# Second half of the output projection and second norm by token tile, two U blocks ahead of query 0, norm weights and keys loaded at the end of the heads

## What is computed

```
x = x + mix @ w_out[l]
x = x + peer_ffn(rms_norm(x, norm2_g[l]), peer_wq[l], peer_keys[l], peer_u[l], peer_v[l])
```

## Time and profile before

| what | value |
|---|---|
| median of three runs | 3324.43 us (3320.78 to 3326.95) |
| span of the profiled execution, first to last instruction | 3318.1 us |
| what lies around the span, by the median | 6.3 us |
| PE busy | 3164.0 us, 95% of the span |
| DVE busy | 2483.5 us, 75% |
| ACT busy | 1336.4 us, 40% |
| POOL busy | 1087.9 us, 33% |

### The profile page before, as it was taken

How to read it: one execution, slowest core, us unless ns; L and a number is a source line. 1 busy time by engine, 2 the same in 40 slices (tenths; PEclk the granted TensorE clock), 3 DMA queues, 4 the chain that set the end, 5 groups by cost and what they waited for, 6 DMA issues and landing times.

```text
span 3318.1 us, 52454 instructions
## 1 busy us (share of the span) xinstructions
PE 3164.0 (95%) x16946; PEld 2781.2 (84%) x16946; DVE 2483.5 (75%) x4220; ACT 1336.4 (40%) x2351; POOL 1087.9 (33%) x621
## 2 busy tenths in 40 slices
PE   7999999999989999999999999999997999999999
PEld 5888799899878888887877877998997888888887
DVE  4554499899688787887645554998996897878876
ACT  4333333355444333343344333333553334343434
POOL 3443354400134333341044434443001333333310
PEclk9999999999999999999999999999998999999999
DMA  3211234588898998998622112445898998989895
GB/s 110 83 51 51 102 128 129 187 301 326 327 343 322 335 340 319 331 336 327 220 103 70 51 57 102 137 134 191 320 329 320 336 344 318 330 321 350 319 336 200
DMA packets 249542, 774.29 MB, mean 233 GB/s; under 512 B 20352, under 2 KB 124928, under 8 KB 216320
## 3 DMA queue, kind: packets, MB, share of 16 engines
q1 hardware_dynamic: 212480, 503.53, 43.4%
q0 software_dynamic: 36864, 268.45, 21.4%
HBM read 689.59 MB, written 82.31 MB: 233 GB/s over the span
## 4 chain that ended last, share of the span: by engine, by line
PE 52%; DVE 14%; issue 13%; DMA 10%; DVEq 7%; ACT 3%; POOL 1%; SPq 0%; ACTq 0%; POOLq 0%
PE PS L471 15%; PE PS L473 15%; PE PS L472 15%; DMA VRAW<-in_peer_v 7%; DVEq L1564 6%; DVE VLO L1550 4%; DVE ROWS L1478 4%; PE PS L757 3%; DVE X L1484 2%; PE PS L651 2%; DMA ROWS<-in_peer_rows,LIST 2%; ACT VHI L1074 1%; DVE WLO L1553 1%; POOL RL L1598 1%; PE PS L713 1%
## 5 line engine op out<-in xcount | busy, mean ns | idle before, releaser
L471 PE MATMUL PS<-XH,RH 128*128 128x384 f32 (+1 forms) x2720 | 979.4, 360 | 17.9 <-DVE XL L1199 9.8
L1598 POOL TENSOR_TENSOR RL<-RAW,RH 128x1024 fp32r<-128x1024 f32 x294 | 728.6, 2487 | 749.7 <-ACT RH L864 749.2
L473 PE MATMUL PS<-XH,RL 128*128 128x384 f32 (+1 forms) x2720 | 953.2, 350 | 0.0
L472 PE MATMUL PS<-XL,RH 128*128 128x384 f32 (+1 forms) x2720 | 952.1, 350 | 0.0
L1632 POOL DMA_INDIRECT ROWS<-in_peer_rows,LIST x256 | 291.2, 1137 | 1315.1 <-DVE X L1484 1283.7
L471 PE MATMUL PS<-VHI,WHI 128*128 128x512 f32 x1536 | 607.1, 395 | 69.8 <-DVE WLO L1553 69.3
L473 PE MATMUL PS<-VHI,WLO 128*128 128x512 f32 x1536 | 603.2, 393 | 0.0
L472 PE MATMUL PS<-VLO,WHI 128*128 128x512 f32 x1536 | 602.9, 392 | 0.0
L471 PEld LDWEIGHTS PS<-XH,RH 128*128 128x128 f32 x2720 | 513.6, 189 | 46.5 <-DVE XL L1199 13.1
L472 PEld LDWEIGHTS PS<-XL,RH 128*128 128x128 f32 x2720 | 514.2, 189 | 27.7
L473 PEld LDWEIGHTS PS<-XH,RL 128*128 128x128 f32 x2720 | 512.3, 188 | 28.7
(11 more groups left out here) (235 smaller groups left out, 3423.7 us busy)
## 6 DMA issues: line engine op xcount, KB each, us to landing
RAW<-in_peer_u SPq DMA_DIRECT2D x256, 512.0 KB, 4.6
VRAW<-in_peer_v SPq DMA_DIRECT2D x256, 512.0 KB, 5.9
RAW<-in_stream SPq DMA_DIRECT2D x128, 512.0 KB, 3.4
route_dram<-STAGE SPq DMA_DIRECT2D x64, 768.0 KB, 7.0
GC<-route_dram SPq DMA_DIRECT2D x64, 768.0 KB, 10.5
gelu_dram<-GS SPq DMA_DIRECT2D x152, 192.0 KB, 4.4
GB<-gelu_dram SPq DMA_DIRECT2D x32, 768.0 KB, 12.5
GEL<-gelu_dram SPq DMA_DIRECT2D x6, 768.0 KB, 7.9
```

The costliest lines, as they stand in the source:

```text
L471: pe.matmul(acc, sh, mh, start=first, stop=False)
L472: pe.matmul(acc, sh, ml, start=False, stop=False)
L473: return pe.matmul(acc, sl, mh, start=False, stop=last)
L1598: pool.tensor_tensor(RL[:, k % 4, :], RAW[:, k % 2, :], RH[:, k % 4, :].bitcast(F32), ALU.subtract).then_inc(S.low_part, 1)
```

## The change

In the second half of the output projection PE goes tile by tile: tiles 0 and 1 over the four blocks, mixed so that a block is first wanted as late as may be, then tile 2, then tile 3. Behind each tile come its sum, norm and transposes, and those of an earlier tile stand between the products of a later one. DVE scales a whole row by the root and by GAIN in one instruction (`norm_tile`); for tile DT the result is XG itself, and ACT scales no rows any more. A tile's eight transposes go into two PSUM banks, four in each, and ACT and DVE split a tile in two instructions each (`split_tile`). Fills 0 and 1, which need tiles 0 to 2 only, stand ahead of query 0, the transposes of tile DT between them. All later fills are two numbers further on beside the same query, so that six fills in place of eight stand between query 15 and the wait for `choice_ready`. GAIN and KEYS are loaded when the last head is stored, behind block 39 in SP's order.

```diff
-                with sp.Fori(0, J_WQ // 4) as i:
...
+                with sp.Fori(0, J_WOUT // 4) as i:
+                    load_stream(i)
+                sp.wait_ge(S.head_stored, count(l, "head_stored", HEADS))
+                sp.dma_start(GAIN[:], gains[l]).then_inc(S.gain_loaded, 16)
+                sp.dma_start(KEYS[:], peer_keys[l]).then_inc(S.keys_loaded, 16)
+                with sp.Fori(J_WOUT // 4, J_WQ // 4) as i:
+                    load_stream(i)
...
-                sp.wait_ge(S.residual_added, count(l, "residual_added", 8))
-                sp.dma_start(KEYS[:], peer_keys[l]).then_inc(S.keys_loaded, 16)
-                sp.dma_start(GAIN[:], gains[l]).then_inc(S.gain_loaded, 16)
...
+                def transpose_tile(t):
+
+                    pe.wait_ge(S.residual_added, count(l, "residual_added", (2, 4, 6, 8)[t]))
+                    pe.wait_ge(S.rows_normed, count(l, "rows_normed", TT + t + 1))
+                    rows = XG if t == DT else XS[1][:, t, :]
+                    for k in range(KD):
+                        m = pe.transpose(PS[:, TILE_BANK[t] + k // 4, k % 4 * P:(k % 4 + 1) * P], rows[:, k * P:(k + 1) * P], IDN[:])
+                        if k % 4 == 3:
+                            m.then_inc(S.norm_transposed, 1)
...
+                for t, kk in ((0, 0), (0, 1), (0, 2), (1, 0), (0, 3), (1, 1), (1, 2), (1, 3)):
+                    if t == 0:
+                        pe.wait_ge(S.low_part, count(l, "low_part", J_WOUT + 4 + kk + 1))
+                    project(t, 1, kk)
+                transpose_tile(0)
+                for kk in range(4):
+                    project(2, 1, kk)
+                transpose_tile(1)
+                for kk in range(3):
+                    project(3, 1, kk).then_inc(S.block_used, 1)
+                transpose_tile(2)
+                project(3, 1, 3)
+                last_block_used(1)
...
-                transpose_norm(1, 8)
-
-                pe.wait_ge(S.keys_loaded, count(l, "keys_loaded", 16))
...
+                pe.wait_ge(S.norm_low, count(l, "norm_low", KD + 5))
+                fill(0, J_WQ, 0, 6, range(0, 4))
+                pe.wait_ge(S.norm_low, count(l, "norm_low", KD + 6))
+                fill(0, J_WQ, 0, 6, range(4, KD))
+                transpose_tile(DT)
+                fill(1, J_WQ + 1, 1, 7)
+                pe.wait_ge(S.norm_low, count(l, "norm_low", 2 * KD))
+                pe.wait_ge(S.keys_loaded, count(l, "keys_loaded", 16))
                 for q in range(4):
-                    n = J_WQ + q if q < 2 else 44 + 3 * q
-                    fills = [(2 * q - 4 + m, n + 1 + m, (n + 1 + m) % 4, 6 + m) for m in range(2)]
-                    query(q, q, n, n % 4, fills if q >= 2 else [], norm=1 if q == 0 else None)
+                    n = J_WQ + 2 + q if q < 2 else 46 + 3 * q
+                    fills = [(2 * q - 2 + m, n + 1 + m, (n + 1 + m) % 4, 6 + m) for m in range(2)]
+                    query(q, q, n, n % 4, fills if q >= 2 else [])
...
-                for f in range(24, FIRST - 2):
+                for f in range(26, FIRST - 2):
...
+                def split_tile(t, half):
+
+                    act.wait_ge(S.norm_transposed, count(l, "norm_transposed", KD + 2 * t + half + 1))
+                    act.activation(XH[:, 4 * half:4 * half + 4, t * P:(t + 1) * P],
+                                   PS[:, TILE_BANK[t] + half, :].rearrange("p (k t) -> p k t", k=4),
+                                   ACT.Copy).then_inc(S.norm_high, 1)
...
+                square_half(0, 1)
                 root(l, 1, 0)
-                scale_rest(l, 1, 0)
...
+                square_half(1, 1)
                 root(l, 1, 1)
...
+                split_tile(0, 0)
+                split_tile(0, 1)
+                square_half(2, 1)
+                split_tile(1, 0)
                 root(l, 1, 2)
+                split_tile(1, 1)
+                hi(0, J_WQ)
+                hi(0, J_WQ + 1)
+                split_tile(2, 0)
+                split_tile(2, 1)
+                square_half(3, 1)
                 root(l, 1, 3)
...
+                hi(0, J_WQ + 2)
...
+                fill_gelu(0, J_WQ, 0, 0)
+                split_tile(DT, 0)
+                split_tile(DT, 1)
+                hi(0, J_WQ + 3)
+                fill_gelu(1, J_WQ + 1, 0, 1)
...
+                def norm_tile(t):
+
+                    dve.wait_ge(S.rms_ready, count(l, "rms_ready", TT + t + 1))
+                    dve.scalar_tensor_tensor(XG[:] if t == DT else XS[1][:, t, :], X[:, t, :], NRM[:, 2, t:t + 1], GAIN[:],
+                                             ALU.mult, ALU.mult).then_inc(S.rows_normed, 1)
...
+                for t in range(2):
+                    add_projected(t, 1)
+                    variance(l, 1, t)
+                    norm_tile(t)
+                split_tile(0)
+                add_projected(2, 1)
+                variance(l, 1, 2)
+                norm_tile(2)
+                split_tile(1)
+                split_tile(2)
+                add_projected(3, 1)
                 variance(l, 1, 3)
...
+                norm_tile(3)
+                split_tile(3)
```

More of the change, by code:

```diff
@@ L341, in _ @@
                 for k in range(2):
-                    load_query(J_U + 22 + k, 14 + k, k)
-                for f in range(24, FIRST):
+                    load_query(J_U + 24 + k, 14 + k, k)
+                for f in range(26, FIRST):
                     load_experts(J_U + f, f, f % 2)
@@ L484, in by_columns @@
                     return m
[L486 to L507, removed]
@@ L665, in _, with project @@
                     two_tiles(j, OH, OL, 0)
[L667 to L675, removed]
-                    for t in range(TT):
[L677 to L682, removed]
+                def project(t, h, kk):
+                    for i in range(2):
+                        k, w, tok = 2 * kk + i, slice(i * 512, (i + 1) * 512), slice(t * P, (t + 1) * P)
+                        m = passes(PS[:, 4 - 4 * h + t, :], XH[:, k, tok], XL[:, k, tok],
+                                   RH[:, kk, w], RL[:, kk, w], k == 0, k == KD - 1)
+                    if kk == 3:
+                        m.then_inc(S.projected, 1)
+                    return m
@@ L701, in fill, with query @@
                         m.then_inc(S.block_used, 1)
-                def query(n, k, block, slot, fills, norm=None):
+                def query(n, k, block, slot, fills):
                     pe.wait_ge(S.low_part, count(l, "low_part", block + 1))
-                    by_columns(2 * (k % 2) if norm is None else 4, slot, norm=norm).then_inc(S.block_used, 1)
+                    by_columns(2 * (k % 2), slot).then_inc(S.block_used, 1)
                     for a in fills[:1]:
@@ L874, in _ @@
                 hi(0, 1)
-                split_norm(0, V_N1)
+                for k in range(KD):
+                    act.wait_ge(S.norm_transposed, count(l, "norm_transposed", k + 1))
+                    act.activation(XH[:, k, :], PS[:, (NORM_BANK + k) % 8, :], ACT.Copy,
+                                   scale=VEC[:, V_N1 + k:V_N1 + k + 1]).then_inc(S.norm_high, 1)
                 for j in range(J_C, J_P):
@@ new lines, in split_tile @@
+                def split_tile(t, half):
[3 more added lines that the diff above has]
+                                   ACT.Copy).then_inc(S.norm_high, 1)
+                for n in range(J_WOUT + 2, J_WOUT + 6):
+                    hi(0, n)
+                act.activation(ROOT[:], ONES[:], ACT.Sqrt)
@@ L1019, in _ @@
                 for k in range(2, 4):
-                    hi(0, J_U + 22 + k)
-                    take_query(12 + k, k, J_U + 20 + k, 2 * (k % 2))
-                for f in range(24, FIRST):
+                    hi(0, J_U + 24 + k)
+                    take_query(12 + k, k, J_U + 22 + k, 2 * (k % 2))
+                for f in range(26, FIRST):
                     if f == FIRST - 3:
@@ new lines, in _ @@
+                for t in range(TT):
+                    add_projected(t, 0)
+                dve.wait_ge(S.gain_loaded, count(l, "gain_loaded", 16))
+                for t in range(2):
[9 more added lines that the diff above has]
+                add_projected(3, 1)
```

152 lines of the change are left out of this document (79 added, 73 removed).

## The result

The changed kernel takes 3300.49 us, the kernel before 3322.53 (medians of 8 runs each, taken side by side): a ratio of 0.9944, 95% interval 0.9924 to 0.9964, 0.56% faster. Later comparisons, on two chips, gave 0.9973 (0.9957 to 0.9989) for the same kernel and 0.9957 (0.9934 to 0.9980) for one with the same schedule and a loop as well placed. The mean of the three is 0.9958, some 14 us. Of the first 22 us a part is thus the spread of runs: those of the kernel before, in one of these comparisons, lie up to 35 us apart (3292.84 to 3327.61).

What follows compares the result with a forecast made beforehand. A DVE chain from first key scores to choice was taken as the bound, PE from 660 on; key scores +2.4, GW -2.0, and the tail gave -0.5 a layer, -1 us in all: 3323.4 from 3324.4, range 3314 to 3332.

Steps and rivals of the forecast that it cites:

- The loads: GAIN and KEYS loaded behind block 39 on SP: cost nothing, and take away DVE's 4.01 us wait for GAIN.
- PE up to the key scores: PE from the projection's second half to query 0's end: work adds to 41.1 us, key scores 2.4 us later.
- The 0.3 us for block 46: Start of the projection's second half: tile 0 wants block 46 at 363.3, POOL has it at 363.58, so PE waits.
- Query 0's old 7.7 us: Query 0 on PE before the change: spread over 7.7 us by missing low parts and slow first instructions; 5.5 expected.
- The norm keeps up: Norm of each tile on DVE and ACT: done under PE's other work, 0.7 us to spare at tile 3, nothing added.
- The second rival: Norm of tile 3 blocked by POOL's low part, held some 2 us more; 3332 us if tile 2 is caught; chance 0.11.
- DVE from the key scores to the choice: DVE's chain behind query 15, with fewer POOL low parts: LIST 1.0 us and GW 2.0 us earlier, counted from query 0.
- The choice, the gather, and what PE is ahead at routing: From the choice on: choice +0.4 us, gather -0.8, result -0.5 a layer; PE stands about 11 us before the choice.
- the first rival: PE is the bound all through: fills moved forward bring PE to the choice 5.9 us earlier a layer, 3312.6; chance 0.14.
- From 660 on PE is the bound: Behind the choice, from 660 us in the first layer, PE was taken to set the time.
- The 6.3 us around the span: Time outside the profiled span, taken as unchanged: a span of 3318.1 goes to about 3317.

Runs made afterwards that it cites:

- the three pairs of equal schedule and different placement: Old schedule without and with sixteen empty DVE instructions (15.1 us), changed kernel with two and eighteen (8.6), early loads without and with sixteen (14.5).
- changed + 2: Changed kernel with two empty DVE instructions a layer ahead of the V stage: 0.9986 of the kernel before, median 3304.53 us.
- changed + 18: Changed kernel with eighteen empty DVE instructions a layer ahead of the V stage: 0.9957 of the kernel before, median 3295.97 us.
- before + 16: Kernel before with sixteen empty DVE instructions a layer ahead of the V stage, nothing else: 0.9961 of the kernel before, median 3294.69 us.
- changed again: The changed kernel as it is, measured again as the mark for later runs: 0.9973 of the kernel before.
- query 0 first: Changed kernel with query 0 put ahead of the two U blocks (fills): 1.0029 of the kernel before.

## Why the prediction was wrong

**The loads.** Costed at nothing, and they delay nothing: right, block 40 is issued 43.8 us ahead of the half in both kernels. But the earlier trace rows were read one block off: the issue at 316.71 is that of block 40, and GAIN's is at 309.77 in the trace after. What they bring was put too low. I took DVE's 4.01 us for GAIN as gone and then spent the gain in the same sum on two U blocks; alone the loads are worth 4.5 us a layer.

**PE up to the key scores.** 2.4 us later was said, 1.9 is the mean of the rows. The 0.3 us for block 46 did not occur. Query 0's old 7.7 us were put down in part to missing low parts; it was the clock, at 0.50 in the row of 392 to 396 us above.

**The norm keeps up.** Right: waits of 0.39 us, a scaling of 1.28 to 1.29 us four times. The second rival, a norm blocked by POOL, did not occur: no low part of POOL ran under a scaling in either layer, so what one would have cost was not seen.

**DVE from the key scores to the choice.** Right in kind: NUMBER 0.29 us, no low part under it. Counted from the key scores LIST comes 1.5 us earlier (said 1.0) and GW 2.5 (said 2.0).

**The choice, the gather, and what PE is ahead at routing.** GW -0.6 (said +0.4), gather -0.9 (said -0.8), routing -0.8 (said -0.5), PE's wait for GW 10.7 (said about 11). In both layers 1.6 us, against 1 in the forecast. By that row the first rival, in which PE is the bound all through, is dead.

**"From 660 on PE is the bound."** This step failed. From it I took everything behind the routing as unchanged, a term of nothing. What the runs showed in its place: in the V stage PE waits for DVE, DVE stands 5.6 to 7.5 us at each of six ways back, and where the change happens to put the loop it does not. The gain lies there: 8.6 to 15 us by the three pairs of equal schedule and different placement. With the 1.6 us of the schedule that makes 10 to 17, and the mean of the three measured ratios is 14. The schedule by itself, at equal placement, gave -0.14% (changed + 2 beside before), -0.04% (changed + 18 beside before + 16, one chip) and +0.12% (changed again beside before + 16, two chips): no difference that can be measured, as forecast. The prediction has no row of the V stage. The list from which the earlier trace rows are taken begins with the row that should have stopped me, the largest of PE's waits, and it lies in that stage:

```profile
PE PS L471 <- DVE WLO L1553: 69.3, 27, 15.9
```

Most of that row has other causes: without the slow ways back it is still 44.8 to 60.0 in six profiles.

**The 6.3 us around the span.** They were a median less the span of one other execution; wherever both are known for one execution, 1.8 us lie around it. The forecast of the time does not rest on it.

What stays open: why 40 us of standing on DVE cost 8.6 us in one pair and 15.1 in another. The V stage of single profiles lasts 754 to 769 us with the slow ways back (eight, mean 761.2) and 750 to 763 without (twelve, mean 756.6): some 9 us for two layers, but one profile of it proves little. PE's waits in the 40 us behind the ways back come to 4.0, 9.6, 3.3 and 2.9 us in the four profiles with slow ones, and to nothing in the ten others. That DVE's later waits for V rows take up part of its 40 us is seen in the rows; where the rest of the price arises was not shown.

## What to carry to other kernels

A change that adds or drops a few instructions moves all code behind it on that engine; before a gain or loss is put down to the schedule, look at the first instruction behind each way back for an "issue" wait of several us, count packets on the instruction queue, and compare with the same code shifted by some empty instructions. Where a loop of a few hundred instructions runs on the engine that others wait for, place it on purpose. And take a change apart: here the smallest part, two loads moved, was worth more than the whole, since the date of the first key scores set the choice as long as PE kept up with the queries behind them.

## What the runs showed of the hardware

A way back of these two loops of DVE costs 0.2 to 0.3 us, or else 2.9 to 3.7 in the loop of the queries and 5.2 to 7.5 in that of the V stage, by the place of the loop alone; two instructions decide. The way back of the whole layer costs 4.0 us in both kernels, and 3.7 to 5.7 over all. With query 0 first PE was granted 1.2 GHz from 385 to 394 us, around and behind waits of 3.67 and 1.49 us, and 24 instructions took 8.4 us in place of 5.5. In the kernel before the clock was the same from 392 to 396 us, behind a wait of 4.30; behind one of 1.08, with early loads, it stayed at 2.4 GHz. Here an idle gap ahead of a stage was paid for again in the stage.
